# A slot table built by matrix products instead of scatters through memory, and expert weights fetched during the routing

## What is computed

```python
    group_probs = jax.nn.softmax((xf @ w_group + b_group).astype(jnp.float32), axis=-1)
    p_group, g_idx = lax.top_k(group_probs, 1)
    e_logits = (xf @ w_expert + b_expert).astype(jnp.float32).reshape(n, N_GROUPS, EXPERTS_PER_GROUP)
    e_logits = jnp.take_along_axis(e_logits, g_idx[:, :, None], axis=1)[:, 0]
    p_exp, e_local = lax.top_k(jax.nn.softmax(e_logits, axis=-1), TOP_K)
    gate = p_group * p_exp / jnp.sum(p_exp, axis=-1, keepdims=True)
    flat_e = (g_idx * EXPERTS_PER_GROUP + e_local).reshape(-1)
    order = jnp.argsort(flat_e)
    tok = order // TOP_K
    group_sizes = jnp.bincount(flat_e, length=N_EXPERTS).astype(jnp.int32)
    xs = xf[tok]
    hid = jax.nn.silu(lax.ragged_dot(xs, w1, group_sizes)) * lax.ragged_dot(xs, w3, group_sizes)
    ys = lax.ragged_dot(hid.astype(xs.dtype), w2, group_sizes) * gate.reshape(-1)[order][:, None].astype(xs.dtype)
    return jax.ops.segment_sum(ys, tok, num_segments=n).reshape(B, T, D)
```

## Time and profile before

| quantity | us |
|---|---|
| median of 3 runs | 3626.59 |
| lowest and highest of them | 3620.15, 3627.68 |
| the profiled execution | 3620.57 |
| its span, first to last instruction | 3618.7 |

### The profile page before, as it was taken

How to read it: one execution, slowest core, us unless ns; L and a number is a source line. 1 busy time by engine, 2 the same in 40 slices (tenths; PEclk the granted TensorE clock), 3 DMA queues, 4 the chain that set the end, 5 groups by cost and what they waited for, 6 DMA issues and landing times. The chain is left out here.

```text
span 3618.7 us, 40957 instructions
## 1 busy us (share of the span) xinstructions
PE 3165.2 (87%) x14897; PEld 2211.0 (61%) x14897; DVE 1517.5 (42%) x1988; ACT 1085.5 (30%) x1457; POOL 1069.3 (30%) x555
## 2 busy tenths in 40 slices
PE   7999999979999979949699897999594599999993
PEld 4656566448888868834344444999442477777772
DVE  2443444431111111146510345444414477787875
ACT  1222222111111112210120122222202477777773
POOL 0000000123333324420000213222000478787874
PEclk9999999989999989969799998999796799999996
DMA  2000010211111132325500104300201799999995
GB/s 106 18 18 18 18 65 1 82 47 47 46 46 46 46 118 97 94 115 181 203 25 0 46 25 165 120 12 1 90 39 50 280 357 373 369 372 366 372 369 220
DMA packets 117904, 458.49 MB, mean 127 GB/s; under 512 B 15153, under 2 KB 16081, under 8 KB 111777
## 3 DMA queue, kind: packets, MB, share of 16 engines
q1 hardware_dynamic: 104242, 409.43, 30.6%
q0 software_dynamic: 8368, 28.65, 2.4%
q10 hardware_dynamic: 5184, 18.88, 1.3%
HBM read 404.29 MB, written 52.52 MB: 126 GB/s over the span
## 5 line engine op out<-in xcount | busy, mean ns | idle before, releaser
L2582 DVE TENSOR_TENSOR moe_w_low<-moe_raw_up,moe_w_high 128x1024 fp32r<-128x1024 f32 x288 | 437.3, 1556 | 160.0 <-ACT moe_w_high L2523 159.8
L2446 POOL TENSOR_TENSOR moe_w_low<-moe_raw_down,moe_w_high 128x1024 fp32r<-128x1024 f32 x144 | 417.2, 2924 | 149.0 <-ACT moe_w_high L2533 149.0
L2523 ACT ACTIVATE moe_w_high<-moe_raw_up 128x1024 fp32r<-128x1024 f32 x288 | 305.1, 1061 | 206.3 <-PE ps L2486 110.8
L89 PE MATMUL ps<-x1T_high,w_up_high 128*128 128x512 f32 x704 | 278.7, 396 | 13.6 <-POOL w_up_low L735 13.6
L89 PE MATMUL ps<-x1T_low,w_up_high 128*128 128x512 f32 x704 | 281.9, 400 | 0.0
L89 PE MATMUL ps<-x1T_high,w_up_low 128*128 128x512 f32 x704 | 276.9, 393 | 0.0
L583 POOL TENSOR_TENSOR res<-res,ln_b 128x1024 f32<-128x1024 f32 x16 | 37.5, 2344 | 781.4 <-DVE res L575 781.4
L251 PE MATMUL ps<-x0T,wqk 128*128 128x512 f32 x512 | 242.0, 608 | 11.1 <-DMA x0T<-in_xT 9.3
L2501 PE MATMUL ps<-moe_w_high,moe_x_high 128*128 128x512 f32 x576 | 229.1, 398 | 5.8 <-DVE moe_x_low L2611 5.8
L2503 PE MATMUL ps<-moe_w_high,moe_x_low 128*128 128x512 f32 x576 | 225.6, 392 | 0.0
L2502 PE MATMUL ps<-moe_w_low,moe_x_high 128*128 128x512 f32 x576 | 225.5, 391 | 0.0
(11 more groups left out here) (406 smaller groups left out, 5911.2 us busy)
## 6 DMA issues: line engine op xcount, KB each, us to landing
moe_raw_up<-in_w SPq DMA_DIRECT2D x288, 512.0 KB, 10.6
moe_raw_down<-in_w SPq DMA_DIRECT2D x144, 512.0 KB, 7.5
w_ada<-in_w_ada SPq DMA_DIRECT2D x48, 512.0 KB, 4.8
w_up<-in_ffn_w_up SPq DMA_DIRECT2D x22, 1024.0 KB, 4.8
w_down<-in_ffn_w_down SPq DMA_DIRECT2D x44, 512.0 KB, 3.5
y_rows<-xT ACTq DMA_DIRECT2D x36, 512.0 KB, 8.3
y_rows<-zero_rows SPq DMA_DIRECT2D x1, 16384.0 KB, 49.3
wqk<-in_attn_wqk SPq DMA_DIRECT2D x8, 1024.0 KB, 4.8
```

The lines of the kernel that those rows point to most:

```text
L89: ins = pe.matmul(out, stationary, moving, start=start and n == 0, stop=stop and n == last)
L2446: pool.tensor_tensor(w_low[:, down_slot(k)], raw_down[:, k], w_high[:, down_slot(k)].bitcast(F32), ALU.subtract).then_inc(down_low, 1)
L2523: act.activation(w_high[:, up_slot(n)], raw_up[:, n], ACT.Copy).then_inc(up_high, 1)
L2582: dve.tensor_tensor(w_low[:, up_slot(n)], raw_up[:, n], w_high[:, up_slot(n)].bitcast(F32), ALU.subtract).then_inc(up_low, 1)
```

## The change

1. **The table by products.** DVE marks for each pair, with comparisons against a list 0 to 127, in which row (`at_row`, 128 wide) and in which block (`at_block`, 48 wide, times the token number) its slot is. PE multiplies the marks of the 16 token columns into one 128x48 result (`tabled`), which is the table. The scatters, the clearing, the read-back and the turn are gone; POOL has nothing to do in the stage.
2. **Fixed first blocks.** Block e, for e below 32, is expert e's first block. Further blocks of an expert with over 128 pairs lie from 32 on. The count becomes 32 + sum of max(ceil(count/128) - 1, 0). The slot of a pair takes five more DVE instructions over 128x256 elements and some small ones. `SLOTS_MIN` becomes 4096, so that `stage_delta` zeroes 2048 rows where it zeroed 4096.
3. **Weights of block 0 in the routing.** Since block 0 belongs to expert 0, SP asks for its 12 pieces in `stage_route`, right behind the small tables; in `stage_experts` it skips them.
4. **The order at the start of stage_experts.** For block 0, ACT raises pieces 0 to 5 ahead of `x_high` and DVE lowers pieces 0 to 3 ahead of `x_low`.

```diff
-SLOTS_MIN = TOP * T
+SLOTS_MIN = EXPERTS * P
...
-            sp.wait_ge(zeroed, 1)
-            sp.dma_start(d["slot_token"].rearrange("(b p) a -> b (p a)", p=P), zeros[:]).then_inc(cleared, 16)
-            sp.wait_ge(scattered, 16 * TOP * TT)
-            sp.dma_start(table[:], d["slot_token"].rearrange("(b p) a -> b (p a)", p=P)).then_inc(read_back, 16)
-
-        @block.gpsimd
...
-                    pool.indirect_dma_start(
-                        d["slot_token"], bass.IndirectOffsetOnAxis(ap=m.slot[:, j, t:t + 1], axis=0),
-                        ids[:, t:t + 1], None).then_inc(scattered, 16)
+            for n in range(UPS):
+                sp.dma_start(m.raw_up[:, n].rearrange("p (k n) -> p k n", k=2),
+                             d["w13"][0, :, n // HT, 2 * (n % HT):2 * (n % HT) + 2]).then_inc(m.up_loaded[n], 16)
+            for k in range(HT):
+                sp.dma_start(m.raw_down[:, k], d["w2"][0, :, k]).then_inc(m.down_loaded[k], 16)
...
-            pe.wait_ge(read_back, 16)
-            pe.transpose(ps[:, 3, 0:BLOCKS], table[:], m.ident[0:BLOCKS, 0:BLOCKS]).then_inc(turned, 1)
+            for j in range(TOP):
+                pe.wait_ge(blocks_marked, j + 1)
+                pe.wait_ge(rows_marked, j + 1)
+                for t in range(TT):
+                    ins = pe.matmul(ps[:, 3, 0:BLOCKS], at_row[:, j, t, :], at_block[:, j, t, :],
+                                    start=j == 0 and t == 0, stop=j == TOP - 1 and t == TT - 1)
+            ins.then_inc(tabled, 1)
...
+            then(dve.tensor_scalar(blocks[:], blocks[:], 0.0, None, ALU.max))
...
+            then(dve.scalar_tensor_tensor(second_on[:], start, EXPERTS - 1.0, experts, ALU.add, ALU.subtract))
...
+            then(dve.tensor_scalar(base[:], place[:], (P - 1.0) / 2, 1.0 / P, ALU.subtract, ALU.mult))
+            then(dve.tensor_scalar(base[:], base[:], ROUND, ROUND, ALU.add, ALU.subtract))
+            then(dve.scalar_tensor_tensor(base[:], base[:], 1.0, row(second_on[:], EXPERTS), ALU.min, ALU.mult))
+            then(dve.tensor_tensor(base[:], base[:], row(experts, EXPERTS), ALU.add))
...
+            then(dve.tensor_scalar(slot_block[:], slot_f[:], (P - 1.0) / 2, 1.0 / P, ALU.subtract, ALU.mult))
+            then(dve.tensor_scalar(slot_block[:], slot_block[:], ROUND, ROUND, ALU.add, ALU.subtract))
+            then(dve.scalar_tensor_tensor(slot_row[:], slot_block[:], -float(P), slot_f[:], ALU.mult, ALU.add))
+
+            for j in range(TOP):
+                then(dve.tensor_tensor(at_block[:, j], row(iota[:, 0:BLOCKS], BLOCKS), along(slot_block[:, j, :], BLOCKS),
+                                       ALU.is_equal))
+                dve.tensor_tensor(at_block[:, j], at_block[:, j], along(ids[:], BLOCKS), ALU.mult
+                                  ).then_inc(blocks_marked, 1)
+                dve.tensor_tensor(at_row[:, j], row(iota[:], P), along(slot_row[:, j, :], P), ALU.is_equal
+                                  ).then_inc(rows_marked, 1)
...
@@ -2405,6 +2419,8 @@
         @block.sync
         def _(sp):
             def load_down(b):
+                if isinstance(b, int) and b == 0:
+                    return
...
             def load(i, s, before):
                 b = 2 * i + s
+                if isinstance(b, int) and b == 0:
+                    return
...
             def step(i, s, before):
                 b = 2 * i + s
-                raise_up(b, 0)
-                raise_up(b, 1)
+                ahead = 2 if before else RING
+                for n in range(ahead):
+                    raise_up(b, n)
...
             def step(i, s, before):
                 b = 2 * i + s
+                ahead = 2 if before else 4
                 lower_up(b, 0)
                 if before:
                     hidden(b - 1, 1 - s)
-                lower_up(b, 1)
+                for n in range(1, ahead):
+                    lower_up(b, n)
```

More of the change, by code:

```diff
@@ L62 @@
 SLOTS = BLOCKS * P
-SLOTS_MIN = TOP * T
+SLOTS_MIN = EXPERTS * P
+HT = DE // P
+UPS = DT
 ROPE_THETA = 10000.0
@@ L2290, in _ @@
                 then(dve.tensor_tensor(carry[:, t + 1, :], carry[:, t, :], total[:, t, :], ALU.add))
-            then(dve.tensor_scalar(blocks[:], carry[:, TT, :], 1.0 / P, (P - 1.0) / P - 0.5 + 0.5 / P,
+            then(dve.tensor_scalar(blocks[:], carry[:, TT, :], 1.0 / P, (P - 1.0) / P - 1.5 + 0.5 / P,
                                    ALU.mult, ALU.add))
             then(dve.tensor_scalar(blocks[:], blocks[:], ROUND, ROUND, ALU.add, ALU.subtract))
+            then(dve.tensor_scalar(blocks[:], blocks[:], 0.0, None, ALU.max))
             then(dve.tensor_copy(ends[:, 0, :], blocks[:]))
@@ L2302, in _ @@
             then(dve.tensor_tensor(start, end, blocks[:], ALU.subtract))
+            experts = iota[:, 0:EXPERTS]
+            then(dve.scalar_tensor_tensor(second_on[:], start, EXPERTS - 1.0, experts, ALU.add, ALU.subtract))
             then(dve.tensor_tensor(place[:], ps[:, 1, 0:TT * EXPERTS].rearrange("p (t e) -> p t e", e=EXPERTS),
                                    carry[:, 0:TT, :], ALU.add))
-            then(dve.scalar_tensor_tensor(place[:], row(start, EXPERTS), float(P), place[:], ALU.mult, ALU.add))
+            then(dve.tensor_scalar(base[:], place[:], (P - 1.0) / 2, 1.0 / P, ALU.subtract, ALU.mult))
+            then(dve.tensor_scalar(base[:], base[:], ROUND, ROUND, ALU.add, ALU.subtract))
+            then(dve.scalar_tensor_tensor(base[:], base[:], 1.0, row(second_on[:], EXPERTS), ALU.min, ALU.mult))
+            then(dve.tensor_tensor(base[:], base[:], row(experts, EXPERTS), ALU.add))
+            then(dve.scalar_tensor_tensor(place[:], base[:], float(P), place[:], ALU.mult, ALU.add))
             for j in range(TOP):
@@ L2322, in _ @@
             dve.memset(m.slot_token[:, BLOCKS:], 0.0)
-            dve.wait_ge(turned, 1)
+            dve.wait_ge(tabled, 1)
             dve.tensor_copy(m.slot_token[:, 0:BLOCKS], ps[:, 3, 0:BLOCKS])
@@ L2340, in two @@
             return [sem(name + "0"), sem(name + "1")]
-        HT = DE // P
-        UPS, RING = DT, 6
+        RING = 6
         gate2 = m.mod[:, 5 * D:6 * D]
-        raw_up = sb("moe_raw_up", [P, UPS, D])
-        raw_down = sb("moe_raw_down", [P, HT, D])
+        raw_up, raw_down = m.raw_up, m.raw_down
         w_high = sb("moe_w_high", [P, RING, D], F32R)
@@ L2360, in stage_experts @@
         hid = [tiles[4][:, 0:DE], tiles[4][:, DE:2 * DE]]
-        up_loaded = [sem(f"moe_up_loaded{n}") for n in range(UPS)]
-        down_loaded = [sem(f"moe_down_loaded{k}") for k in range(HT)]
+        up_loaded, down_loaded = m.up_loaded, m.down_loaded
         indexed, gathered, stored = (two("moe_" + n) for n in ("indexed", "gathered", "stored"))
@@ L2552, in step @@
                 act.activation(x_high[:], two_banks(ps, 0), ACT.Copy).then_inc(x_high_out, 1)
-                for n in range(2, RING):
+                for n in range(ahead, RING):
                     raise_up(b, n)
@@ L2849, in second_block @@
         m.slot_token = sb(s1, "slot_token", [P, BLOCKS + 2], U32)
+        m.raw_up = sb(s1, "moe_raw_up", [P, UPS, D])
+        m.raw_down = sb(s1, "moe_raw_down", [P, HT, D])
+        m.up_loaded = [nc.alloc_semaphore(f"moe_up_loaded{n}") for n in range(UPS)]
+        m.down_loaded = [nc.alloc_semaphore(f"moe_down_loaded{k}") for k in range(HT)]
         stage_route(nc, d, m)
```

43 lines of the change are left out of this document (19 added, 24 removed).

## The result

The changed kernel takes 3603.98 us (median of 4 runs, 3600.86 to 3608.70) against 3626.23 for the kernel before (median of 4). The two medians lie 22.2 apart. The ratio is 0.9949, its 95% interval 0.9937 to 0.9961: faster by 0.51% (the medians alone would give 0.61%), clear of the 0.2% that can be told from no change. The forecast was 3608.1, 18.5 less than before. The times agree with the forecast better than its terms do, as the trace shows.

What follows compares the result with a forecast made beforehand. The prediction saw a chain of scatters, read-back and turn, then a second chain starting the experts' stage. Terms 17.2 - 0.1 + 1.4 = 18.5 us, from the median 3626.59, gave 3608.1; range 3596 to 3618.

Steps and rivals of the forecast that it cites:

- three signs: Signs of error: the copy waits over 2 us for PE, logit products start late, or the period moves over 0.1.
- Up to the slots: Routing on DVE before the slots are ready: added small and 256-element instructions cost 2.03 us.
- Marks: Routing on DVE after the slots: three small instructions, 0.63 us, and marks for two ranks, 4.72 us.
- PE beside them: Routing's 16 table products on PE: at 0.25 us each, the last eight are hidden under DVE's 2.8 us.
- Weights behind the small tables: Weight pieces on SP's queue right behind the last small table: DMA engines have room, cost 0.1 us.
- Start of the experts' stage: From gather to first upward product: ACT's high part no longer stands behind a piece just come, gain 1.4 us.
- The gather's issue: POOL's gather issue beside DVE's lowering: up to 0.8 us lost, set with a quicker landing at zero together.
- Block 0: Block 0's 48 upward products on PE: unchanged, with the clock left as it is.
- slow products: First rival: the 16 table products take 0.61 us each, ending 4.6 behind DVE; gain 13.9, time 3612.7; chance 0.08.
- weights in front: Rival: small tables land only after the 12 weight pieces, routing starts 15.2 us late; time 3623.3; chance 0.04.
- slower loop: Rival: POOL's low parts in the block loop take 0.2 us longer each; time 3636; chance 0.04 including more blocks.
- more blocks: Rival: an expert without a pair still gets its block, costing 39.5 us; time 3647.6; chance 0.04 including slower loop.

Runs made afterwards that it cites:

- e7: Changed kernel with the old order at the start of the experts' stage (two pieces ahead of the rows' parts on ACT and DVE); stretch 71.33 us.
- e8: Changed kernel with the table made by scatters through memory again; 3620.91 us against 3621.83 for the kernel before, ratio 0.9997.
- e9: Changed kernel with the twelve weight pieces asked for ahead of the five small tables on SP; 3621.18 us in one run, against 3620.26.
- e6: Changed kernel without early weights and with the old order, so products and fixed first blocks only; stretch 74.20 us.

## Why the prediction was right or wrong

The direction, the mechanism (a chain through memory, replaced by a shorter one) and the time were right. The size was right in part by luck: the terms sum to 18.5, the stretch shows 13.3 to 15.0, and the medians happened to lie 22.2 apart in this comparison and 15.6 and 14.4 in the next two. By two of the three signs that the prediction itself names it was wrong: the copy waits for over 2 us for PE, and the logit products start late. What the stretch shows is nearer to the 13.9 of its first rival than to its own sum. Step by step:

- **Up to the slots, 2.03.** Measured from the logits, 17.81 before and 19.81 after: 2.00. Right.
- **Marks, 0.63 + 4.72.** 2807.07 to 2812.10: 5.03. Right, 0.3 too high since instructions without a wait behind them overlap.
- **Tail on DVE, 2.8.** 2812.10 to 2814.74: 2.64. Right.
- **PE beside them, hidden at 0.25 a product.** This step failed. The 16 products took 7.03, 0.44 each, and T came 2.46 after DVE was ready. I had read the row of L2206 as two products of 0.61; it is one product of the code, which the profile gives as x2. A float32 product is two instructions, and the turns, which I took as the nearer row, are one each. Counting instructions against the code's lines would have given two of at most 0.25 for a product, 16 x 0.5 from 2804.5 on, and a wait of up to 2.8. The fp32r marks show it: 16 instructions, no wait.
- **Weights behind the small tables, 0.1.** Mis-sized: 1.9 by the means of the landings, 2.8 in the profile of the result. The rest of the 4.2 there, 1.4, is one long issue on SP that also comes without early weights. The order, from which I let the rival fall, holds: asked for ahead of the tables, the weights delay them by 17 us, 6.9 of them by waiting behind the pieces. But directly behind them they still delay them. I took "goes first" for "is not touched", and took the room in the DMA engines (0.02) for an answer; there was room in the changed kernel too, 0.12 from 2771 to 2774, while the table was late.
- **Start of the experts' stage, 1.4.** Measured 2.81, and 2.56 and 2.62 in the other two profiles of the changed kernel. High and low part follow the turn as forecast (turn's end 2824.85, first product 2827.22), and ACT's six pieces were done at 2824.24, in time by 0.6. The turn now starts at T+5.47 where it was T+6.65, which is 1.2 of it, and the first product follows 1.6 sooner behind the turn's start, where 1.4 were forecast. The term was low because the gather landed in 4.3 where it had taken 5.6: alone in the DMA engines it is quicker, the bound of 4.3 that I had worked out and set against a loss that did not come. With weights asked for beside it it takes 5.6 (before) or 6.4 (table alone, fixed blocks).
- **The gather's issue.** It took 1.05, not 1.79, because DVE begins to lower only as it ends. The second gather's issue, beside DVE's lowering, took 1.80. With the old order (e7), where DVE has lowered its two pieces by then, the same issue took 0.98, the last of these rows:

```profile
2818.49 1.05 POOL L2457 DMA_INDIRECT xT<-h_rows,slot_index  x1 [0.34 <-issue]
...
2822.10 1.80 POOL L2457 DMA_INDIRECT xT<-h_rows,slot_index  x1
```

```profile
2827.95 0.98 POOL L2457 DMA_INDIRECT xT<-h_rows,slot_index  x1
```

- **Block 0, 0.** +0.49 in the result's profile, ten instructions at the low clock (1.2 GHz) where there were eight; +0.3 and +0.5 in the other two profiles of the changed kernel. Over all the kernels block 0 takes 12.59 to 13.75, so this term needs an allowance of about 1, which I had not made; where it was over 13.3, 1.5 came back in the next blocks.
- **The loop, the halved zeroing, the number of blocks, all 0.** Right: 691.97 for 692.00, and 36 blocks. The zero transfer fell from 49.3 to 29.2 and nobody had waited for it.

The rivals: slow products came true in half their size (2.5 of 4.6), weights in front in an eighth (1.9 of 15.2). The slower loop and more blocks did not come. What the forecast lacked is the view of the parts apart: it gave the fixed first blocks a cost (2.0) and the early weights a gain (1.4 - 0.1) and did not say that the two together lose. By the profiles they do: the table alone gains 16.1 to block 35, the whole change 13.3 to 15.1; the times can't tell the two apart.

## What to carry to other kernels

A table of a few thousand entries that is scattered into memory and read back costs an issue of POOL for every column and a round trip, here 27.6 us from the slots to the finished table, 22.6 of them with DVE idle; comparisons and products that add up one-hot marks make it in 7.8 with fp32r marks, 10.3 with float32, and the marks should be in a format whose product is one instruction. Before transfers are moved into a stage because the DMA engines are idle there, look at which small transfer gates that stage, and let the large ones wait for it. When a change has several parts, price each alone: here, by the profiles, one part carries all of the gain, and two others pay only once the marks are in fp32r, when the shorter owners' table counts (17.6 to block 35 against 16.3 for the table alone), and more when the weights wait for the small tables (18.1 and 18.4). And end a measured stretch where the clock has settled: block 0 and the blocks behind it traded 1.5 us.

## What the runs showed of the hardware

- A product of float32 data is two instructions on PE, of fp32r data one, and with 48 columns at the low clock (granted clock 0.50 there) each takes 0.22 to 0.23 us: 32 in 7.03, 16 in 3.74.
- Twelve transfers of 512 KB, asked for right behind a 64 KB one on the same queue, raised its landing from a mean of 3.6 to 5.5 us; asked for ahead of it, they landed first. With a 24 KB transfer between it and them its landing was near 3.4 (e8). The Trainium skill (DMA: Bandwidth & Descriptors, section "Queues, rings and completion order") has the order; the order shows in e9; the hold-up from behind the section doesn't give.
- An indirect transfer's issue on POOL took 0.98 to 1.05 us with DVE idle and 1.80 beside `TENSOR_TENSOR` instructions of DVE with two inputs in SBUF. POOL's copy of 128 row numbers went from 0.18 to 1.26 beside them. The first scatter took 1.68 where such an instruction of 1.75 us lay beside it, and 1.04 in the kernel with scatters kept, where it did not. The Trainium skill (SBUF — State Buffer, section "Who interferes with whom") lets such a DVE instruction contend with GpSimd's reads only, and leaves descriptor writing free by inference. The copy agrees. The issue reads its row numbers from SBUF too (`slot_index`), which the prediction passed over when it put the loss at 0 by that section, so which of the two slows it no run here shows.
- From 1 to 4 us behind block 0's end PE is busy for 0.7 us in all. In the changed kernel the granted clock then went from 1.00 (2.4 GHz) to 0.50 (1.2 GHz) for about 3 us, and all ten profiles with block 0 in 12.59 to 13.22 show a mean of 0.83 over the ten microseconds; in the four in which the clock had risen later in block 0 (13.36 to 13.75) it stayed at 1.00, in e6 over the same pause of PE.
- The work ahead of the change took up to 10 us more or less from one profile to the next. The cause is open.
